# Moving the rounding copy of the MLP's hidden tiles from ScalarE to VectorE, in a hybrid attention, SSM and MLP block

## The reference

```
h = rms_norm(x, norm_g[2]) * (1 + sc_f) + sh_f
y = square(relu(h @ w_up)) @ w_down        # w_up 1024 x 4096, w_down 4096 x 1024
x = x + gt_f * rms_norm(y, norm_g[3])
```

## Time and profile before

| | us |
|---|---|
| median of 3 runs | 2836.55 (2836.28 to 2839.34) |
| the profiled execution, its own time | 2836.28 |
| its span, from first to last instruction | 2834.5 |
| PE busy in it | 2566.9 (91%) |
| DVE, ACT, POOL busy | 1332.6, 702.4, 693.1 |

### The profile page before, as it was taken

One profiled execution on the slowest core, in us unless ns is written; L12 is line 12 of the kernel. 1 busy time (PEld: TensorE's weight loads), 2 busy tenths in 40 slices (PEclk: granted clock), 3 DMA queues, 4 the chain that ended last, 5 costly groups with the idle time before them and its releaser, 6 DMA issues.

```text
span 2834.5 us, 34170 instructions
## 1 busy us (share of the span) xinstructions
PE 2566.9 (91%) x12630; PEld 2051.9 (72%) x12630; DVE 1332.6 (47%) x1910; ACT 702.4 (25%) x1402; POOL 693.1 (24%) x281
## 2 busy tenths in 40 slices
PE   6999998678799999899899889998869999999997
PEld 2866885344478778678778768887858787787875
DVE  2249999954532723713623645554332222313226
ACT  3153210044412322412322321002442121211212
POOL 1111320000112421512512513222122222233220
PEclk9999999889999899999999989999979999999999
DMA  6000433411411021021021044341221111111103
GB/s 233 31 30 31 155 141 119 163 58 65 126 34 31 16 75 45 15 75 45 16 75 45 1 178 143 116 141 61 90 74 36 55 45 44 44 44 44 57 32 119
DMA packets 133212, 208.86 MB, mean 74 GB/s; under 512 B 7316, under 2 KB 104948, under 8 KB 132084
## 3 DMA queue, kind: packets, MB, share of 16 engines
q1 hardware_dynamic: 117680, 158.77, 17.0%
q10 hardware_dynamic: 15428, 48.57, 4.4%
HBM read 165.38 MB, written 41.94 MB: 73 GB/s over the span
## 4 chain that ended last, share of the span: by engine, by line
PE 65%; issue 14%; DVE 12%; ACT 4%; PEld 2%; DMA 1%; DVEq 1%; ACTq 0%; PEldq 0%; SPq 0%
PE ps L558 63%; PEld ps L558 2%; DVE state L1548 1%; DVE score L1452 1%; DVE top L1448 1%; PE ps L760 1%; DVE decay L1534 1%; DVE c_out L1517 1%; DVE c_out L1519 1%; DVE acc L1584 1%; ACT decay L1197 0%; DVE y_t L1557 0%; DVE y_t L1555 0%; DVE y_t L1554 0%; DMA ada<-in_ada_w_dram 0%
## 5 line engine op out<-in xcount | busy, mean ns | idle before, releaser
L558 PE MATMUL ps<-a_hi,w_hi 128*128 128x512 f32 x1728 | 686.2, 397 | 40.9 <-issue 17.6
L558 PE MATMUL ps<-a_lo,w_hi 128*128 128x512 f32 x1728 | 679.8, 393 | 0.0
L513 POOL CAST w_hi<-raw 128x2048 fp32r<-128x2048 f32 x86 | 166.7, 1939 | 1893.4 <-PE ps L558 1072.9
L558 PE MATMUL ps<-a_hi,w_lo 128*128 128x512 f32 x1728 | 537.6, 393 | 0.0
L558 PEld LDWEIGHTS ps<-a_hi,w_hi 128*128 128x128 f32 x1728 | 329.0, 190 | 121.1 <-issue 36.6
L515 POOL TENSOR_TENSOR w_lo<-raw,w_hi 128x2048 fp32r<-128x2048 f32 x86 | 404.0, 4698 | 6.9
L558 PEld LDWEIGHTS ps<-a_lo,w_hi 128*128 128x128 f32 x1728 | 329.1, 190 | 70.0 <-issue 2.1
L558 PEld LDWEIGHTS ps<-a_hi,w_lo 128*128 128x128 f32 x1728 | 328.6, 190 | 69.4
L1645 DVE TENSOR_TENSOR x_tm<-x_tm,ps 128x1024 f32<-128x1024 f32 x120 | 146.5, 1221 | 463.9 <-PE ps L558 463.9
L558 PE MATMUL ps<-w_hi,a_hi 128*128 128x256 f32 (+1 forms) x896 | 259.3, 289 | 27.3 <-DVEq L322 14.4
L558 PE MATMUL ps<-w_lo,a_hi 128*128 128x256 f32 (+1 forms) x896 | 257.9, 288 | 0.0
(11 more groups left out here) (240 smaller groups left out, 3201.7 us busy)
## 6 DMA issues: line engine op xcount, KB each, us to landing
raw<-in_w_in_dram SPq DMA_DIRECT2D x31, 1024.0 KB, 5.0
ada_raw<-in_ada_w_dram SPq DMA_DIRECT2D x16, 1024.0 KB, 5.2
raw<-in_w_up_dram SPq DMA_DIRECT2D x16, 1024.0 KB, 5.4
raw<-in_w_down_dram SPq DMA_DIRECT2D x16, 1024.0 KB, 4.8
gates<-gate_d SPq DMA_DIRECT2D x12, 1024.0 KB, 4.9
act_raw<-acts_d ACTq DMA_DIRECT2D x20, 512.0 KB, 6.2
ada<-in_ada_w_dram SPq DMA_DIRECT2D x8, 1024.0 KB, 20.4
acts_d<-c_out ACTq DMA_DIRECT2D x16, 512.0 KB, 4.8
```

What stands on the lines that cost most here:

```text
L513: nc.gpsimd.tensor_copy(hi, src).then_inc(hi_made, 1)
L558: return nc.tensor.matmul(o, a, b, start=start, stop=stop)
```

## The change

The copy into `u_hi` leaves ACT's `hidden` and is now DVE's, in `u_part`, ahead of the subtraction. The semaphore `u_rounded` goes; DVE waits for the square (`u_squared`) instead. In `chunk`, the four u_part(c+1, j) stand ahead of add_down(c, t) for t = 0 to 3, where they stood behind add_down(c, t) for t = 2 to 5. ACT no longer waits for the down block that last read `u_hi` (DVE's `down_before` covers that). In the loop DVE's own count is told its eight links a turn.

```diff
-            def hidden(n, c, b, extra=0, first=False):
+            def hidden(n, c, extra=0, first=False):
                 act.wait_ge(w_used[n % 2], n // 2 + 1 + extra)
-
-                if not first:
-                    act.wait_ge(w_used[0], c + N_MLP // 2)
                 for j in range(4):
                     if not first:
                         act.wait_ge(u_split, c * 4 + (j - 3))
-                    m, q = divmod(j, 2)
                     nc.scalar.activation(u_tmp[j][:, :], ps[:, j, :], ACT.Relu).then_inc(up_out, 1)
                     act.wait_ge(up_out, c * 4 + (j + 1))
                     nc.scalar.activation(u_tmp[j][:, :], u_tmp[j][:, :], ACT.Square).then_inc(u_squared, 1)
-                    act.wait_ge(u_squared, c * 4 + (j + 1))
-                    nc.scalar.copy(u_hi[b][:, m, q * 512:q * 512 + 512], u_tmp[j][:, :]).then_inc(u_rounded, 1)
...
             def u_part(c, b, j):
-                dve.wait_ge(u_rounded, c * 4 + (j + 1))
+                dve.wait_ge(u_squared, c * 4 + (j + 1))
+                V.link(ve.tensor_copy(u_hi[b][:, m, r], u_tmp[j][:, :]))
                 ve.tensor_tensor(u_lo[b][:, m, r], u_tmp[j][:, :], u_hi[b][:, m, r].bitcast(F32), ALU.subtract).then_inc(u_split, 1)
...
-            def chunk(c, b, first=False, down_before=None):
+            def chunk(c, b, last=False, first=False, down_before=None):
...
                 for t in range(NT):
+                    if t < 4 and not last:
+                        u_part(c + 1, 1 - b, t)
                     add_down(c, t, first)
-                    if 2 <= t < 6:
-                        u_part(c + 1, 1 - b, t - 2)
...
             with dve.Fori(1, NC // 2 - 1) as i:
+                V.enter(i - 1, 8)
                 chunk(i * 2, 0, down_before=(w_used[0], i * 2 + (N_MLP // 2 + 1)))
                 chunk(i * 2 + 1, 1, down_before=(w_used[0], i * 2 + (N_MLP // 2 + 2)))
+                V.leave(NC // 2 - 2)
```

More of the change, by code:

```diff
@@ L303, in hybrid_block @@
         z_square, z_var, z_root = sem("z_square"), sem("z_var"), sem("z_root")
-        up_out, u_squared, u_rounded, u_split, down_done, down_out = (
-            sem(n) for n in ("up_out", "u_squared", "u_rounded", "u_split", "down_done", "down_out"))
+        up_out, u_squared, u_split, down_done, down_out = (sem(n) for n in ("up_out", "u_squared", "u_split", "down_done", "down_out"))
         block = ctx.enter_context(nc.Block())
@@ L1306, in hidden @@
                     nc.scalar.activation(u_tmp[j][:, :], u_tmp[j][:, :], ACT.Square).then_inc(u_squared, 1)
-                    act.wait_ge(u_squared, c * 4 + (j + 1))
-                    nc.scalar.copy(u_hi[b][:, m, q * 512:q * 512 + 512], u_tmp[j][:, :]).then_inc(u_rounded, 1)
-            hidden(N_MLP, 0, 0, first=True)
+            hidden(N_MLP, 0, first=True)
             with act.Fori(0, NC // 2 - 1) as i:
-                hidden(N_MLP + 1, i * 2 + 1, 1, extra=i * 2)
-                hidden(N_MLP + 3, i * 2 + 2, 0, extra=i * 2)
-            hidden(N_ALL - 3, NC - 1, 1)
+                hidden(N_MLP + 1, i * 2 + 1, extra=i * 2)
+                hidden(N_MLP + 3, i * 2 + 2, extra=i * 2)
+            hidden(N_ALL - 3, NC - 1)
             for t in range(NT + 1):
```

## The result

The changed kernel takes 2912.6 us (median of 4 runs, 2907.81 to 2915.97) against 2837.95 us before (median of 4 runs), 74.7 us more. The ratio is 1.0245 with the 95% interval 1.023 to 1.0261: slower by about 2.5%, some 70 us. The two differences don't contradict each other: the result holds 22 runs of the changed kernel in all, with a mean of 2907.9 us. The time moved as forecast in direction and place, and it is 10 to 15 us above the forecast's point of 2897.5, inside its range. The profiled execution has a span of 2908.0 us, 73.5 more than before.

A forecast was written before the change was run, and what follows sets the result against it. PE was taken to set the pace, so only a new wait of PE could move the time. 2836.3 + 45.6 (waits for DVE) + 17.6 (clock) - 2.0 (shorter first pause) = 2897.5 us, range 2874 to 2914.

The forecast's parts named there:

- What bounds the kernel: MLP: PE sets the pace, busy 44.64 of 45.00 us; only a new wait of PE can move the time.
- Part 1: After the first up block: without ACT's copy, PE's wait for relus shrinks by 2.0 us, bounds 0 and 3.7.
- the upper bound's mechanism (3.7): After the first up block: the shorter pause also brings PE's clock back earlier, by 1.6 us.
- Part 2: Start of 15 down blocks: POOL holds DVE's first copy and subtraction, tile 2 starts 3.0 us late; 45.6 us.
- Part 3: After the new pauses in down blocks: PE's clock falls in 11 of 15, 1.6 us each; 17.6 us.
- The bound of 24: Upper bound for the clock's loss after the 15 pauses in down blocks: 24 us.
- B: Down blocks: DVE's subtraction gets in ahead of POOL's, tile 3 starts 1.7 late, no clock fall; 2860; chance 0.09.
- C: Down blocks: DVE's copy waits for POOL's whole subtraction, stall 3.6 us a chunk; 2912; chance 0.06.
- D: Down blocks: PE's waits come but its clock never falls; 2880; chance 0.12 with its neighbours.
- E: Down blocks: new copy and subtraction don't wait for POOL, only the first pause's gain stays; 2834.3; chance 0.05.

The follow-up runs named there:

- e1_late: Changed kernel with the old order: DVE's copy and subtraction behind add_down for t = 2 to 5 again; 2832.15 us against 2834.92 before the change.
- e2_early_sub: Kernel before with the new order only: copy stays on ACT, subtractions ahead of add_down for t = 0 to 3; 2849.85 us, ratio 1.0057.
- e3_pool_held: Changed kernel with POOL's split at the end of up(c+1) held back until chunk c+1's four u_parts are done; 2832.14 us, ratio 0.9989.
- e4_fill: Changed kernel with 12 further matmuls on PE ahead of tile 2 in 15 down blocks; 2879.83 us, ratio 1.0155.
- e7_after: The changed kernel itself, run again beside the runs with added matmuls; 2909.98 us, ratio 1.0256 to the kernel before.

## Why the prediction was right, and where it was off

- **What bounds the kernel.** Right: PE's work did not change, ACT's relief was worth nothing in the 15 later chunks, and the time moved by a new wait of PE at tile 2.
- **Part 1, the first pause.** The wait fell by 2.0 us, as forecast. The clock gave about 1 us more: the step from the first to the second chunk's relu shrank by 3.0 (30.93 to 27.92). After the pause of 4.1 us the matmuls were 0.43 us apart for about 3.5 us, after the one of 6.1 for 5.3. That was the upper bound's mechanism (3.7), which I had priced at nothing. e1_late, where this part stands alone, is 2.8 us faster.
- **Part 2, the hold.** Right. Forecast and measured, from the first relu: copy's end 2.16 and 2.22, POOL's end 6.62 and 6.66, subtraction's end 7.16 and 7.22, addition from 7.1 and 7.14, tile 2 8.35 and 8.41; 45.6 us in all, and measured 15 times 3.10, 46.5 us, from tile 2's start, of which 44.0 are new idle time in the wait list (45.4 less 1.4). One step of it isn't tested by the changed kernel: POOL's subtraction was to wait for DVE's copy and end 4.46 after it, but it ends at 6.66 as it did before, so the copy took nothing from it that can be seen. e2_early_sub shows that wait: POOL's subtraction ends 4.50 us after DVE's there. e1_late and e3_pool_held take either party out of the collision and the loss is gone.
- **Part 3, the clock.** The mechanism was right and the term mis-sized: 11 falls at 1.6 us, 17.6, where it was 15 falls, nine at 1.60 and six at 2.88, so about 32 (30 by e4_fill against e7_after). The difference, 12 to 14 us, is what puts the time 10 to 15 us above the point. The ledger closes: from the first relu to the end the MLP takes 75.1 us more than before, and 46.5 + 31.7 - 3.0 makes 75.2. I had taken the share of falls from between two sorts of pauses, 2.1 and 2.9 us, though the one pause near 2.9 that I had a row of was followed by one; and I had priced each at the one stretch of the earlier trace rows, without asking whether a stretch can be longer. The bound of 24 was too low for the same reason. A longer one stood in the trace before: after the 6.1 us pause behind the first up block the matmuls were 0.43 us apart from 2117.69 to 2122.97, 5.3 us. By the rule of the Trainium skill, "TensorE: Matmul & The Clock Gate", section "HAM oscillation — how this bites in real kernels", in which every turn's wait throttles PE again, all 15 would fall, and all 15 did. At my price of 1.6 it would have given 2904. But the waits in that section's loop are of 3 to 5 us, so at 2.93 it was stretched, and the pause of 2.89 us in e2_early_sub, not followed by a fall, speaks against "every time".
- **Rivals.** B (DVE's subtraction first) did not happen in the changed kernel, but does happen in 14 of 15 chunks of e2_early_sub, where the subtraction asks 0.3 us earlier. C was excluded by the copy's 0.92 us. D, the waits without the clock, is what e4_fill makes: 2879.83 measured, 2880 forecast. E did not happen, since the copy and the subtraction are held; what it describes, part 1 alone, is what e1_late and e3_pool_held reach (2832, 2.8 us under the kernel before).
- **Still open.** Why six of the stretches at the lower clock are twice as long as the nine others, when the pause is the same 2.93 us in all. The two profiles of the changed kernel (e7_after has five long ones and ten short) show one part of an answer: in 9 of their 30 chunks tile 2's first matmul is still 0.50 us long and the fall comes a little later, and there the stretch is always short; where that matmul already takes 0.80, 11 are long and 10 short. Open too is why the clock did not fall after the 2.89 us in e2_early_sub, and why the first subtraction asks 0.07 us later there. It is the chunk in which the changed kernel's copy asks late as well, at 1.73 in place of 1.30.

## What to carry to other kernels

Before an elementwise step is moved to VectorE, look at what GpSimd does at that moment, not at VectorE's busy share: the copies and subtractions between SBUF tiles seen here exclude each other, and the later one loses the whole rest of the other. Put such work behind the additions that TensorE waits for, or hold GpSimd back where it has time to spare; one of the two was enough here. And price a pause of TensorE with the slow stretch that can follow it: here that added another two thirds to the pauses themselves.

## What the runs showed of the hardware that was not expected

- The turn between VectorE and GpSimd goes by who asks first, to within 0.06 us: recorded 0.06 us ahead of GpSimd's subtraction, VectorE's takes 0.69 us; recorded in the same hundredth (once), 5.15 us.
- Twelve added matmuls in each of 15 pauses, 180 in all, made the kernel 30 us faster: with idle time of 0.2 us in place of 2.9 TensorE stays at its upper clock.
- Four added matmuls do nearly as well (2885.49 against 2879.83): at 2.0 us idle, 3 of 15 pauses were followed by a fall.
- A pause of almost the same length need not cost the same: after 2.93 us the clock fell 30 times in 30, for a short stretch or one twice as long, and after 2.89 us in the same place of another kernel, seen once, it did not fall.
